# A trunk layer's FFN in split float32: seven of its eleven 512-wide hidden blocks computed by a Strassen scheme on half of K

## The reference

```
def _swiglu(h, w1, w3, w2):
    return (jax.nn.silu(h @ w1) * (h @ w3)) @ w2
...
    for i in range(DEPTH):
        mod = c_act @ ada_w[i] + ada_b[i]
        ...
        h = x * (1.0 + sc_f) + sh_f
        y = _swiglu(h, ffn_w1[i], ffn_w3[i], ffn_w2[i])
        x = _layer_norm(DEEPNORM_ALPHA * x + (1.0 + g_f) * y, ln2_g[i], ln2_b[i])
```

## Time and profile before

| | us |
|---|---|
| median of 3 runs | 2193.56 (2192.49 to 2194.15) |
| span of the profiled execution | 2191.0 |
| PE busy | 2139.0 (98%) |
| DVE busy | 1596.9 (73%) |
| ACT busy | 990.1 (45%) |
| POOL busy | 105.1 (5%) |

### The profile page before, as it was taken

One profiled execution on the slowest core, in us unless ns is written; L12 is line 12 of the kernel. 1 busy time (PEld: TensorE's weight loads), 2 busy tenths in 40 slices (PEclk: granted clock), 3 DMA queues, 4 the chain that ended last, 5 costly groups with the idle time before them and its releaser, 6 DMA issues.

```text
span 2191.0 us, 24820 instructions
## 1 busy us (share of the span) xinstructions
PE 2139.0 (98%) x9557; PEld 1744.3 (80%) x9557; DVE 1596.9 (73%) x1792; ACT 990.1 (45%) x1291; POOL 105.1 (5%) x208
## 2 busy tenths in 40 slices
PE   5799999999999999999999999999999999999999
PEld 2378887888888888888788888878888888888887
DVE  6789999777777777778877666878775555455566
ACT  1077646444443444443544455554444433444443
POOL 2101100000000000000000000000000000000000
PEclk9999999999999999999999999999999999999999
DMA  9999997889998898999589788958987765666773
GB/s 387 418 364 362 363 388 285 276 292 341 337 340 319 320 340 322 318 350 361 193 287 331 264 273 282 338 175 290 332 295 226 234 194 191 214 212 213 219 239 124
DMA packets 177064, 635.90 MB, mean 290 GB/s; under 512 B 20385, under 2 KB 51377, under 8 KB 150705
## 3 DMA queue, kind: packets, MB, share of 16 engines
q1 hardware_dynamic: 147298, 427.93, 56.0%
...
...
## 4 chain that ended last, share of the span: by engine, by line
PE 86%; DMA 6%; DVE 6%; ACT 2%; issue 1%; POOL 0%; ACTq 0%; SPq 0%; DVEq 0%; POOLq 0%
PE ps L1862 53%; PE ps L1868 27%; PE ps L1879 3%; DMA gate<-in_ada_w 3%; DMA raw<-in_mla_w_o 1%; DVE wlo L1167 1%; DMA ada_head<-in_ada_w 1%; DVE ada_w L1204 1%; DVE gate L1204 1%; DMA ada_w<-in_ada_w 1%; DMA raw<-in_mla_w_uv 1%; PE ps L2091 0%; ACT whi L710 0%; DVE ada_head L1204 0%; PE ps L2121 0%
## 5 line engine op out<-in xcount | busy, mean ns | idle before, releaser
L1167 DVE TENSOR_TENSOR wlo<-raw,whi 128x1024 fp32r<-128x1024 f32 (+1 forms) x717 | 867.1, 1216 | 513.8 <-ACT whi L710 512.7
L710 ACT ACTIVATE whi<-raw 128x1024 fp32r<-128x1024 f32 (+1 forms) x717 | 756.1, 1056 | 1033.8 <-PE ps L1868 952.4
L1862 PE MATMUL ps<-whi,hT_hi 128*128 128x512 f32 x1880 | 585.7, 393 | 1.5 <-DVE hT_lo L1595 1.5
L1862 PE MATMUL ps<-whi,hT_lo 128*128 128x512 f32 x1880 | 579.5, 389 | 0.0
L1868 PE MATMUL ps<-wlo,hT_hi 128*128 128x512 f32 x1880 | 502.7, 389 | 0.0
L1862 PEld LDWEIGHTS ps<-whi,hT_lo 128*128 128x128 f32 x1880 | 352.9, 188 | 74.0
L1868 PEld LDWEIGHTS ps<-wlo,hT_hi 128*128 128x128 f32 x1880 | 352.9, 188 | 73.7
L1862 PEld LDWEIGHTS ps<-whi,hT_hi 128*128 128x128 f32 x1880 | 350.1, 188 | 72.9 <-DVE hT_lo L1595 2.0
L1204 DVE CUSTOM_DVE_ANT_0 ada_w<-ada_w,c_bc,cols 128x2048 f32<-128x2048 f32 x145 | 339.8, 2345 | 16.4 <-ACT c_bc L1050 8.4
L1862 PE MATMUL ps<-whi,uT_hi 128*128 128x512 f32 x656 | 202.0, 389 | 0.0
L1862 PE MATMUL ps<-whi,uT_lo 128*128 128x512 f32 x656 | 201.9, 389 | 0.0
...
## 6 DMA issues: line engine op xcount, KB each, us to landing
raw<-in_ffn_w SPq DMA_DIRECT2D x528, 512.0 KB, 4.7
ada_w<-in_ada_w POOLq DMA_DIRECT2D x145, 1024.0 KB, 7.6
raw<-in_fox_w_in SPq DMA_DIRECT2D x96, 512.0 KB, 5.3
ada_head<-in_ada_w POOLq DMA_DIRECT2D x16, 1024.0 KB, 20.3
raw<-in_mla_w_o SPq DMA_DIRECT2D x32, 512.0 KB, 8.6
raw<-in_fox_w_o SPq DMA_DIRECT2D x32, 512.0 KB, 5.5
gate<-in_ada_w POOLq DMA_DIRECT2D x12, 1024.0 KB, 9.0
ada_low<-in_ada_w POOLq DMA_DIRECT2D x10, 1024.0 KB, 10.4
```

What stands on the lines that cost most here:

```text
L710: nc.scalar.activation(split_hi(pl.unit)[:, 0:n], raw[:, s, 0:n], ACT.Copy).then_inc(hi_ready, 1)
L1167: nc.vector.tensor_tensor(split_lo(pl.unit)[:, 0:n], raw[:, s, 0:n], split_hi(pl.unit)[:, 0:n].bitcast(F32), ALU.subtract).then_inc(lo_rea ...
L1862: nc.tensor.matmul(ps[:, 2 * pair + t, 0:width], a[:, t * P:(t + 1) * P], w_hi, start=(first and c == 0 and a is hi), stop=False)
```

## The change

In blocks 4 to 10 of the second layer the first 8 of the 16 chunks of K are computed by a Strassen (Winograd) scheme of seven products in place of eight, in two groups (MIXES = 2) of four chunks. In a group the row tiles of h (t) and its two chunk pairs (x) form a 2 x 2 matrix, and so do the rows of K and the pair `w1`, `w3`. The other half of K stays as it was: four units of `w1`, four of `w3`.

- A fast unit is one weight operand and one 128-row stationary operand, 6 matmuls (`operand`). A group has seven, so a block has 14 fast and 8 plain units, 22 in place of 16, and 180 matmuls in place of 192.
- Three of a group's weight operands are plain loads (B11, B21, B22). Four are sums or differences of them (T1, T3, T2, T4). POOL makes each by a DMA that adds the next weight onto what lies in the raw slot (`accum_op=ALU.add`, new line L810), once DVE has split what lay there; ACT waits for it (`sum_in`).
- The mixed rows of h (S1 to S4) are made once, in block 3 (`mix_inputs`, `mix_low`), in the space of `c_bc` and `ada_w`. These must be done with then: the modulation goes after every second unit in the first half of block 3, and also runs on to the end of the second half of block 2.
- Two more raw slots (`raw_more`) lie over `c_bc` too, and are loaded only after `mix_ready`. `raw_slots` gives each unit its slot.
- ACT and DVE combine seven partial products from PSUM (`fast_block`), and PE waits for their reading.

The diff, cut to its core:

```
+FAST_FROM = 4
+MIXES = 2
+FAST_GROUPS = range(MIXES)
+PLAIN_UNITS = range(2 * MIXES, PAIRS)
+FAST_BLOCKS = range(FAST_FROM, sum(FF_PASSES))
+S1, S2, S3, S4 = range(4)
+W1, W3 = "ffn_w1", "ffn_w3"
+def fast_units():
+    half = len(PLAIN_UNITS) // 2
+    w1 = [("plain", j, W1, j, None) for j in PLAIN_UNITS]
+    w3 = [("plain", j, W3, j, None) for j in PLAIN_UNITS]
+    def mixes(kind, name, which, onto=None):
+        return [(kind, g, name, 2 * g + which, onto) for g in FAST_GROUPS]
+    return (mixes("B11", W1, 0) + mixes("B21", W1, 1) + mixes("B22", W3, 1) + w1[:half]
+            + mixes("T1", W3, 0, "B11") + mixes("T3", W3, 0, "B22") + w1[half:]
+            + mixes("T2", W3, 1, "T1") + w3[:half]
+            + mixes("T4", W1, 1, "T2") + w3[half:])
+FAST_UNITS = fast_units()
+FAST_COUNT = len(FAST_UNITS)
+AT = {kind: 1 + max(n for n, u in enumerate(FAST_UNITS) if u[0] == kind) for kind in ("B11", "T1", "T2", "T3", "T4")}
+MORE_RAW = 2
+MIX_AT = 2
...
-                s = pl.unit % RING
-                if pl.unit >= RING:
-                    sp.wait_ge(lo_ready, pl.unit - RING + 1)
-                sp.dma_start(raw[:, s, 0:source.shape[-1]], source).then_inc(raw_in[s], 16)
+                n = pl.unit
+                if RAW_FREE[n]:
+                    sp.wait_ge(lo_ready, RAW_FREE[n])
+                if RAW_SLOT[n] >= RING:
+                    sp.wait_ge(mix_ready, 1)
+                sp.dma_start(raw_of(n)[:, 0:source.shape[-1]], source).then_inc(raw_in[RAW_SLOT[n]], 16)
 ...
+                    for kind, g, name, j, onto in FAST_UNITS:
+                        if onto:
+                            pool.wait_ge(lo_ready, RAW_FREE[n])
+                            pool.dma_start(raw_of(n), A[name][1, i * PAIRS + j], accum_op=ALU.add
+                                           ).then_inc(sum_in[kind == "T3"][g], 16)
+                        n += 1
...
+            def fast_block(n, i):
+                b = i - FAST_FROM
+                units(AT["B11"] + 4)
+                act.wait_ge(units_used, pl.pe - 4)
+                act.wait_ge(u_flipped, U_BLOCKS + i)
+                nc.scalar.activation(silu_all[:, 0, :], ps[:, 0, :], ACT.Copy).then_inc(first_copied, 1)
+                units(AT["T1"] - AT["B11"] - 4)
+                act.wait_ge(units_used, pl.pe)
+                nc.scalar.activation(u[:, 1, :], ps[:, 1, :], ACT.Copy).then_inc(fifth_copied, 1)
+                units(AT["T3"] - AT["T1"])
+                if i > sum(FF_PASSES[:n]):
+                    u_high(1, n, i - 1)
+                units(AT["T4"] + 1 - AT["T3"])
+                act.wait_ge(left_done, b + 1)
+                nc.scalar.activation(silu_all[:, :, :], silu_all[:, :, :], ACT.Silu).then_inc(fast_silu, 1)
+                units(FAST_COUNT - AT["T4"] - 1)
...
+            def fast_block(n, i):
+                b = i - FAST_FROM
+                units(AT["T3"])
+                if i > sum(FF_PASSES[:n]):
+                    u_low(1, n, i - 1)
+                units(AT["T2"] - AT["T3"])
+                dve.wait_ge(units_used, pl.pe)
+                dve.wait_ge(first_copied, b + 1)
+                chain(nc.vector.tensor_tensor(u[:, 0, :], silu_all[:, 0, :], ps[:, 2, :], ALU.add))
+                nc.vector.tensor_tensor(silu_all[:, 1, :], u[:, 0, :], ps[:, 3, :], ALU.add).then_inc(sixth_read, 1)
+                units(1)
+                dve.wait_ge(fifth_copied, b + 1)
+                dve.wait_ge(sixth_read, b + 1)
+                chain(nc.vector.tensor_tensor(u[:, 0, :], u[:, 1, :], u[:, 0, :], ALU.subtract))
+                mark(nc.vector.tensor_tensor(u[:, 1, :], u[:, 1, :], silu_all[:, 1, :], ALU.subtract))
+                units(AT["T4"] - AT["T2"] - 1)
+                dve.wait_ge(units_used, pl.pe)
+                own()
+                nc.vector.tensor_tensor(silu_all[:, :, :], silu_all[:, :, :], ps[:, 4:6, :], ALU.add
+                                        ).then_inc(left_done, 1)
+                units(FAST_COUNT - AT["T4"])
+                dve.wait_ge(units_used, pl.pe)
+                nc.vector.tensor_tensor(u[:, :, :], u[:, :, :], ps[:, 6:8, :], ALU.add).then_inc(right_read, 1)
+                dve.wait_ge(right_read, b + 1)
+                dve.wait_ge(fast_silu, b + 1)
+                chain(nc.vector.tensor_tensor(u[:, :, :], silu_all[:, :, :], u[:, :, :], ALU.mult))
+                flip(1, i, u)
...
+            def operand(bank, stationary, first, end):
+                s = pl.unit % RING
+                pe.wait_ge(hi_ready, pl.unit + 1)
+                for c, (hi, lo) in enumerate(stationary):
+                    for a in (hi, lo):
+                        nc.tensor.matmul(ps[:, bank, :], a, whi[:, s, c * NB:(c + 1) * NB],
+                                         start=(first and c == 0 and a is hi), stop=False)
+                pe.wait_ge(lo_ready, pl.unit + 1)
+                for c, (hi, lo) in enumerate(stationary):
+                    ins = nc.tensor.matmul(ps[:, bank, :], hi, wlo[:, s, c * NB:(c + 1) * NB],
+                                           start=False, stop=(end and c == UC - 1))
+                ins.then_inc(units_used, 1)
+                pl.unit += 1
...
+            def fast_block(i):
+                b = i - FAST_FROM
+                pair_free(pl.block)
+                pair_free(pl.block + 1)
+                if b == 0:
+                    pe.wait_ge(mix_ready, 1)
...
+                    if l == 1:
+                        done = sum(i < made - U_BLOCKS for i in FAST_BLOCKS)
+                        for read in (first_copied, fifth_copied, sixth_read, left_done, right_read):
+                            pe.wait_ge(read, done)
```

More of the change, by code:

```diff
@@ new lines, with unit_kinds @@
+FAST_UNITS = fast_units()
[3 more added lines that the diff above has]
+MIX_AT = 2
+U_OUT_AFTER, U_BACK_AFTER = 7, 12
+RAWS = RING + MORE_RAW
+TOTAL = NAIVE + len(FAST_BLOCKS) * (FAST_COUNT - 2 * PAIRS)
+LAST_DOWN = TOTAL - 4 * FF_PASSES[-1] * 4 // UC
+FFN_1 = NAIVE - 3 * D_FF // P * 4 // UC
+def unit_kinds():
+    kinds, first = [None] * FFN_1, 0
+    for nb in FF_PASSES:
+        for i in range(first, first + nb):
+            kinds += FAST_UNITS if i in FAST_BLOCKS else [None] * (2 * PAIRS)
+        kinds += [None] * (4 * 4 * nb // UC)
+        first += nb
+    return kinds
@@ new lines, with raw_slots @@
+UNIT_KINDS = unit_kinds()
+assert len(UNIT_KINDS) == TOTAL
+FAST_START = next(n for n, kind in enumerate(UNIT_KINDS) if kind)
+def raw_slots():
+    slots, before, loads = [], [], []
+    last = [-1] * RAWS
+    used = [0] * RAWS
+    sums = collections.Counter()
+    held = {}
+    for n, kind in enumerate(UNIT_KINDS):
+        if n < FAST_START:
+            s = n % RING
+        elif kind and kind[4]:
+            s = held.pop((kind[4], kind[1]))
+        else:
+            s = min((m for m in range(RAWS) if m not in held.values()), key=lambda m: last[m])
+        if kind and any(u[4] == kind[0] for u in FAST_UNITS):
+            held[kind[0], kind[1]] = s
+        slots.append(s)
+        before.append(last[s] + 1)
+        last[s] = n
+        if kind and kind[4]:
+            sums[kind[0] == "T3", kind[1]] += 1
+            loads.append(sums[kind[0] == "T3", kind[1]])
+        else:
+            used[s] += 1
+            loads.append(used[s])
+    return slots, before, loads
@@ L566, in u_back, with load_fast @@
                                      ).then_inc(u_moved[b % 2], 16)
+            def load_fast(first, i):
+                for n, (kind, g, name, j, onto) in enumerate(FAST_UNITS):
+                    if onto:
+                        pl.unit += 1
+                        continue
+                    load(A[name][1, i * PAIRS + j])
+                    if i > first and n == U_OUT_AFTER:
+                        u_out(1, i - 1)
+                    if i > first and n == U_BACK_AFTER:
+                        u_back(1, i - 1)
             def load_ffn(l):
@@ L571, in load_ffn @@
                     for i in range(first, first + nb):
+                        if l == 1 and i in FAST_BLOCKS:
+                            load_fast(first, i)
+                            continue
                         if (l, i) == (0, 0):
@@ L1028, in ffn @@
                             u_high(l, n, first + i - 1)
-                        units(2 if (l, n, i) == (0, 0, 0) else PAIRS)
+                        if l == 1 and first + i == FAST_FROM - 1:
+                            units(MIX_AT)
+                            act.wait_ge(mix_summed, 1)
+                            nc.scalar.activation(s_hi[:, :, :, :], s_32[:, :, :, :], ACT.Copy).then_inc(mix_high, 1)
+                            units(PAIRS - MIX_AT)
+                        else:
+                            units(2 if (l, n, i) == (0, 0, 0) else PAIRS)
                         if (n, i) == (0, nb - 1):
@@ L1137, in _ @@
             pl = Place()
-            total = sum(PROJ) + 1 + 2 * (4 * PAIRS + 3 * D_FF // P * 4 // UC)
+            total = TOTAL
```

(28 more changed lines are left out.)

124 lines of the change are left out of this document (114 added, 10 removed).

## The result

The changed kernel takes 2266.39 us (median; 2265.93 to 2267.59) beside 2193.41 us for the kernel before on the same chip (2192.49 to 2194.15). The ratio is 1.0332, with a 95% interval from 1.0318 to 1.0347. The forecast was 2205.5 us, in a range from 2190 to 2224. Its sign was right and its size was not: 73 us were lost instead of 12.

The account below looks back on a forecast made before the run. PE was taken to bound the kernel. -19.0 + 8.5 + 11.4 + 0.5 + 10.5 = +11.9 us on the span of 2191.0 gives 2202.9; with 2.56 us to the runs' median, 2205.5 us, range 2190 to 2224.

Parts of the forecast that it names:

- What bounds the kernel before: Last 541 us: PE bounds, so a matmul less is time less while ACT, DVE, SP and DMA engines keep up.
- Step 1: Blocks 4 to 10: 12 matmuls fewer in each, 84 x 0.2267 = 19.0 us removed; a block lasts 40.8 us.
- Step 2: Entry to block 4: PE waits for DVE's multiplication of block 3, behind splits whose loads need `mix_ready`; 8.5 us.
- Step 3: Start of each pass's down product and of block 6: three PE waits of 3.8 us for bank readers, 11.4 us.
- the ring: Fast block's chain: transpose, store, read-back, unit 13's load, splits, unit 18's adding DMA, DVE to the next transpose; 42.9 us.
- Step 4: PE's granted clock falls behind the wait at block 4's entry, costing 0.5 us; nothing taken behind waits of 3.8 us.
- Step 5: Fast blocks: the ring takes 42.9 us against PE's 40.8; five blocks pay 2.1 us each, 10.5 us.
- Step 6: DMA engines in a fast block: 1.25 us per 512 KB, an adding DMA costing two plain loads, 40 of 40.8 us busy.
- DMA engines become the bound: Rival, chance 0.12: an adding DMA costs three plain loads, 50 us a block, 2259 us; decides from c of 2.3 up.
- Hidden at no cost: First half of block 3: two modulation tiles brought forward, 4.7 us, covered by DVE's waits for ACT.
- Faster: Rival, chance 0.10: no long entry wait at block 4, as `mix_ready` comes early, and the ring is hidden; 2188 us.
- the ring has slack: Rival, chance 0.22: adding DMAs land in 3.3 to 5 us, the ring stays under 40.8 us; 2194 to 2197 us.

Follow-up runs that it names:

- experiment 2: The changed kernel without the 56 adding DMAs and ACT's waits for them, weight sums left out: 2211.08 us, ratio 1.0074.
- experiment 4: The changed kernel with the read-back issued after unit 13's load instead of before it (U_BACK_AFTER 13 for 12): 2249.31 us, ratio 1.025.
- experiment 1: The changed kernel with its 56 adding DMAs made plain loads of the same size, queue and waits, weight sums left out: 2231.44 us, ratio 1.0169.
- experiment 3: The kernel of experiment 2 with 48, 15, 15 and 15 matmuls nobody reads ahead of PE's four long waits: 2201.14 us, ratio 1.003.

## Why the prediction was right or wrong

**What bounds the kernel before: right.** PE did; without the adding DMAs a matmul less was time less, to 0.01 us a block (experiment 2).

**Step 1, the removed matmuls, 19.0 us: right.**

**Step 2, the entry wait, 8.5 us: place and chain right, 2.3 us short.** The chain is as written. From the timeline of DVE and SP in after:

```profile
1617.28 2.35 DVE L1373 CUSTOM_DVE_ANT_0 ada_w<-ada_w,c_bc,cols 128x2048 f32<-128x2048 f32 x1 [1.63 <-DMA ada_w<-in_ada_w]
...
1624.41 2.28 DVE L1816 TENSOR_TENSOR mix<-hT_hi,hT_lo 128x2048 f32<-128x2048 f32 x1
...
1633.55 2.28 DVE L1831 TENSOR_TENSOR s_lo<-s,s_hi 128x2048 fp32r<-128x2048 f32 x1
...
1635.86 0.80 SPq L598 DMA_DIRECT2D raw_more<-in_ffn_w  x2
...
1645.96 1.23 DVE L1336 TENSOR_TENSOR wlo<-raw,whi 128x1024 fp32r<-128x1024 f32 x1 [0.41 <-ACT whi L850]
...
1647.10 1.28 DVE L1914 TENSOR_TENSOR u<-silu,ps 128x512 f32<-128x512 f32 x2
```

`mix_inputs` was put at 1620.0 and began at 1624.4, because DVE had waited for a modulation tile, and ACT 4.7 us for a unit (split at 1619.12). The tiles brought forward were costed as DVE time alone. It is likely that their transfers of 1 MB also delayed the units; no run separates that. From there on the steps are close to what was worked out: 5.1 us to the end of the mix, 3.6 us for the first landing, then 1.24 to 1.64 us a unit. The wait was 12.5 us in experiments 2 and 4, so it differs by some 2 us from kernel to kernel.

**Step 3, three waits of 3.8 us: right without POOL's loads, short with them.** They are 4.0, 4.0 and 3.7 us in experiment 2. In after the two ahead of the down products are about 8 us. The sum took terms 3 and 5 as independent, but the late loads on POOL's queue make these waits longer: 14.4 us for the two even when those loads are plain (experiment 1), and 16.2 when the ring is cut (experiment 4). The same counter at the fifth unit of the other fast blocks, said to be hidden, costs 6.9 us in five waits, and nothing in experiment 2.

**Step 4, the clock, 0.5 us: wrong by a factor of 20.** "Behind 3.8 us I take nothing" was a choice that no row bore out. Experiment 2 has 13.0 us outside the waits, and experiment 3 gets 9.9 us back by keeping PE busy through them. The windows say the same for one wait: 2.2 to 2.6 us lost, more than half as much again as the wait of 3.7 or 4.0 us itself.

**Step 5, the ring and its effect, 10.5 us: the step that failed.** The ring and its order were right; its length was put at 42.9 us and is 51.1. Term by term, predicted and measured (block 8):

| | predicted | measured |
|---|---|---|
| transpose's end to unit 13's load | 7.1 | 9.6 |
| its landing | 5.6 | 8.7 |
| splits 13, 14 | 3.4 | 3.4 |
| adding DMA, issue to the next split | 7.7 | 7.0 |
| high split of 18 | 1.1 | 1.1 |
| DVE to the end of the transpose | 18.0 | 21.3 |

The disputed term, unit 18's adding DMA, was well put. The one behind it was left out: unit 19's lands 9.1 us after its issue, and DVE waits 2.42 of its 21.3 us for its split (and 0.94 for another, which stood behind ACT's silu). The plain transfers were put too short: their durations came from a stretch at 335 GB/s, in which nothing added. With plain loads in place of the adding ones (experiment 1) the same turn takes 43.4 us, close to the 42.9: 7.8 to unit 13's load, 6.8 for its landing, 5.1 for POOL's load on the chain. So the adding DMAs lengthened the others.

"Block 4's transpose is early and block 6 has nothing to read back, so five blocks pay" was wrong as well: from block 4's first matmul to the end of block 5's right addition are 101.9 us, and from block 6's first to block 10's 254.4, in all 356.3 against 7 x 40.8 = 285.6. These 70.7 us hold the pass ends; the prediction had 18.1 for both. Some 50 of them, 7 x (47.9 - 40.8), are there by the DMA engines' time alone, whatever the ring, so that this step failed through the next one.

With 14.5 for the entry and block 6's start and -19.0 for the matmuls, 66.2 of the 72.9 us on the span are placed. Of the other 6.7, 1.7 lie ahead of block 4 (PE ends block 3 at 1637.7 in place of 1636.0), 0.9 between the two last additions and PE's start behind them, and 4.1 in the down products and what follows. There the first unit takes 4.35 us in the first pass and 5.1 in the second, in place of 2.72, behind the two waits of 8 us; the granted clock around the second one (2110 to 2160 us) is 0.86.

**Step 6, the engines' time, 40 us a block: c right, the unit price wrong, and this is the root of the miss.** With c of 2 in hand, 1.25 us per 512 KB was taken from a stretch of large loads at 420 GB/s. In a block it is 1.52 us. A third of the packets there are under 2 KB (3040 of 8930), but which transfer is dear was not measured by itself. At 1.52 us, 16 + 8 x 1.94 = 31.5 units are 47.9 us, and that decides against the change before any ring is looked at. No new run was needed to see it. The kernel before pays even more per unit in its own blocks, 1900 to 2100 us:

```profile
q1 hardware_dynamic: 17212, 45.41, 70.4%
```

These are 86.6 transfers' worth, 0.704 x 200 / 86.6 = 1.63 us each. At that price c of 2 makes 52 us a block, and the engines' time passes PE's 40.8 us from c of 1.14 up (2.1 at the prediction's price). The rival "DMA engines become the bound" gave 2259 us, nearest to the result. Its bound was the right one, but it came near by luck: its price was wrong (c of 3), the condition it named, c above 2.3, wasn't met, and the waits and the clock, which it took as small, make up the rest.

**Hidden at no cost: wrong in part**, as said under step 2. **"Faster" and "the ring has slack"**: the entry wait is real, and landings of 3.3 to 5 us do not occur for adding DMAs (5.3 us is the least).
